# The last 14 weight transfers of each round, split in two by rows

## The reference, cut to what matters

```python
def _moe(h, router_w, router_b, wg, wu, wd):
    logits = (h @ router_w + router_b).astype(jnp.float32)
    top_v, top_i = lax.top_k(logits, MOE_TOPK)
    top_w = jax.nn.softmax(top_v, axis=-1)
    gates = jnp.sum(top_w[..., None] * jax.nn.one_hot(top_i, N_EXPERTS, dtype=jnp.float32), axis=-2)
    out = jnp.zeros_like(h)
    for e in range(N_EXPERTS):
        out = out + gates[..., e:e + 1] * _swiglu(h, wg[e], wu[e], wd[e])
    return out
```

## Time and profile before

| | |
|---|---|
| three runs | 1885.35, 1886.6 and 1887.86 us |
| median | 1886.6 us |
| the profiled execution, first to last instruction | 1888.6 us |
| mean granted clock of PE | 0.974 of full speed |
| PE busy | 1778.0 us, 94% of the span |
| bytes moved | 541.92 MB |

### The profile page before, as it was taken

How to read it: one execution, slowest core, us unless ns; L and a number is a source line. 1 busy time by engine, 2 the same in 40 slices (tenths; PEclk the granted TensorE clock), 3 DMA queues, 4 the chain that set the end, 5 groups by cost and what they waited for, 6 DMA issues and landing times.

```text
span 1888.6 us, 28344 instructions
## 1 busy us (share of the span) xinstructions
PE 1778.0 (94%) x11337; PEld 1307.8 (69%) x11338; DVE 483.9 (26%) x1052; ACT 276.5 (15%) x567; POOL 353.6 (19%) x215
## 2 busy tenths in 40 slices
PE   7999999999999999999999989989999998999896
PEld 4888788778888788888885857565554443444443
DVE  1595535310000286322322001102100100101101
ACT  2104433010000210534011000000000100000001
POOL 2807241569998000000000000000000000000000
PEclk8999999999999999999989999979999999999999
DMA  9745464367765444445458979898998999999994
GB/s 397 259 156 201 151 232 139 129 251 281 266 246 194 177 145 152 134 145 168 178 208 365 416 286 401 346 419 350 418 414 337 412 421 417 419 418 418 416 421 178
DMA packets 86831, 541.92 MB, mean 287 GB/s; under 512 B 8752, under 2 KB 21072, under 8 KB 21840
## 3 DMA queue, kind: packets, MB, share of 16 engines
q1 hardware_dynamic: 67824, 490.24, 65.7%
q0 software_dynamic: 5760, 41.95, 6.0%
q10 hardware_dynamic: 13024, 6.82, 1.2%
HBM read 537.89 MB, written 1.08 MB: 285 GB/s over the span
## 4 chain that ended last, share of the span: by engine, by line
PE 84%; DMA 7%; issue 3%; SPq 2%; DVE 2%; ACT 2%; ACTq 0%; DVEq 0%
PE ps L799 22%; PE ps L1247 12%; PE ps L876 8%; PE ps L893 8%; PE ps L1395 6%; PE ps L1286 6%; PE ps L900 4%; PE ps L1416 3%; PE ps L1325 3%; DMA sq<-in_moe_units 3%; SPq L597 2%; DMA aring<-in_moe_units 2%; DMA misc<-in_moe_units 1%; PE ps L1357 1%; DMA proj<-in_ada_units 1%
## 5 line engine op out<-in xcount | busy, mean ns | idle before, releaser
L799 PE MATMUL ps<-hT,ring 128*128 128x256 f32 x1984 | 438.0, 382 | 1.0 <-ACT hT L1518 1.0
L799 PEld LDWEIGHTS ps<-hT,ring 128*128 128x128 f32 x1984 | 376.7, 191 | 56.1 <-issue 5.1
L701 POOL TENSOR_TENSOR aring<-aring,ccol 128x2048 f32<-128x2048 f32 x40 | 144.5, 3612 | 208.8 <-DVE scan L1941 65.8
L707 POOL TENSOR_TENSOR aring<-aring 128x1024 f32<-128x1024 f32 x80 | 151.3, 1892 | 6.3
L893 PE MATMUL ps<-hT,ring 128*128 128x256 f32 x672 | 146.7, 379 | 0.0
L1247 PE MATMUL ps<-ring,hT 128*64 128x256 f32 (+2 forms) x1152 | 131.7, 364 | 7.8 <-issue 5.6
L893 PEld LDWEIGHTS ps<-hT,ring 128*128 128x128 f32 x672 | 127.0, 190 | 16.9
L1247 PEld LDWEIGHTS ps<-ring,hT 128*64 128x64 f32 (+2 forms) x1152 | 75.0, 133 | 59.5 <-issue 37.9
L2286 DVE TENSOR_TENSOR proj<-proj,ps 128x256 f32<-128x256 f32 (+2 forms) x28 | 14.6, 521 | 352.5 <-PE ps L1247 352.5
L1926 DVE SCALAR_TENSOR_TENSOR misc<-cpad,par,misc 128x256 f32<-128x256 f32 x240 | 102.7, 507 | 0.0
L876 PE MATMUL ps<-proj,ring 128*128 128x256 f32 x384 | 83.2, 379 | 0.0
(11 more groups left out here) (399 smaller groups left out, 1969.0 us busy)
## 6 DMA issues: line engine op xcount, KB each, us to landing
ring<-in_moe_units SPq DMA_DIRECT2D x144, 1024.0 KB, 19.4
ring<-in_dense_units SPq DMA_DIRECT2D x121, 1024.0 KB, 5.0
aring<-in_moe_units SPq DMA_DIRECT2D x48, 1024.0 KB, 18.8
proj<-in_moe_units SPq DMA_DIRECT2D x48, 1024.0 KB, 20.2
aring<-in_ada_units POOLq DMA_DIRECT2D x40, 1024.0 KB, 6.6
extra<-in_moe_units SPq DMA_DIRECT2D x24, 1024.0 KB, 18.2
scan<-in_moe_units SPq DMA_DIRECT2D x24, 1024.0 KB, 21.2
misc<-in_moe_units SPq DMA_DIRECT2D x24, 1024.0 KB, 21.6
```

The lines of the kernel that those rows point to most:

```text
L701: last = g.tensor_tensor(w, w, ccol[:, :].unsqueeze(2).broadcast_to([P, KT, 256]), ALU.mult)
L707: last = g.tensor_tensor(dst, w[:, 0:half_k, :], w[:, half_k:2 * half_k, :], ALU.add)
L799: last = mm(ps[:, n % 2, j * SEQ:(j + 1) * SEQ], wide(s)[:, k, j * P:(j + 1) * P], hT[:, k, :], start=(k == 0), stop=(k == KT - 1))
```

## The change

It concerns the last 14 units of each round, 154 to 167, by `late` 0 to 13. Each is now sent as two transfers, rows 0 to `cut` and rows `cut` to 128, right after one another from the same queue and after the same single wait. `cut` is 8 times the entry of `LOW_ENGINES`: 120, 112, 104, 96, 88, 80, 64, and then seven times 120. Both transfers raise the slot's semaphore by 16, so that the slot counts 13 fills of 16 in a round instead of 12, and `arrived` asks for one more fill for the last unit of each slot. Nothing that is computed changes, nor the bytes that are moved.

```diff
+ENGINES = 16
+LOW_ENGINES = (15, 14, 13, 12, 11, 10, 8) + (15,) * 7
...
-                sp.dma_start(eslot[slot], moe_units[ds(expert, 1), unit].rearrange("e p n -> p (e n)")
-                             ).then_inc(efull[slot], 16)
+                source = moe_units[ds(expert, 1), unit].rearrange("e p n -> p (e n)")
+                late = piece.first_unit + u - (MEMBERS * UNITS - EXP_SLOTS)
+                if late < 0:
+                    sp.dma_start(eslot[slot], source).then_inc(efull[slot], 16)
+                    return
+                cut = P // ENGINES * LOW_ENGINES[late]
+                sp.dma_start(eslot[slot][0:cut, :], source[0:cut, :]).then_inc(efull[slot], 16)
+                sp.dma_start(eslot[slot][cut:P, :], source[cut:P, :]).then_inc(efull[slot], 16)
...
                 def arrived(key):
                     stream = piece.first_unit + AT[key]
-                    pe.wait_ge(efull[stream % EXP_SLOTS],
-                               p * (16 * (MEMBERS * UNITS // EXP_SLOTS)) + 16 * (stream // EXP_SLOTS + 1))
+                    fills = stream // EXP_SLOTS + 1 + (stream >= MEMBERS * UNITS - EXP_SLOTS)
+                    pe.wait_ge(efull[stream % EXP_SLOTS], p * (16 * (MEMBERS * UNITS // EXP_SLOTS + 1)) + 16 * fills)
                     return stream % EXP_SLOTS
```

## The result

| | before | after |
|---|---|---|
| median | 1887.12 us (4 runs, 1885.35 to 1887.86) | 1969.15 us (4 runs, 1964.33 to 1973.41) |
| profiled execution | 1888.6 us | 1969.6 us |

A forecast was written before the change was run, and what follows sets the result against it. Saturated transfers were taken as the bound, with PE following landings and one engine late. Relieving it in the last round gave -6 us, the first round and SP nothing: 1886.6 - 6 = 1880.6 us, range 1877 to 1897.

The forecast's parts named there:

- What bounds the kernel: Expert phase: transfers saturated at 420 GB/s, PE follows the landings, one lone engine works 10 us longer at the end.
- The price of a row: Late units: an 8 KiB row takes an engine 0.312 us, so 14 rows more cost 4.4 us.
- collisions: Rival, late units: two engines write into the same part of on-chip memory and halve each other; slower, chance 0.24.
- midway 3.75 us a unit: Collision rival's price midway between no and all conflicts: a late unit takes 3.75 us instead of 2.5.
- 17.5 us: Collision rival's midway cost for the 14 late units of one round.
- midway case of 1915: Collision rival at its midway price over both rounds: up to +28 us, ending at 1915.
- The first round: First round's late units: 4.4 us more on engines 0 to 7, covered by 5.4 us idle; cost nothing.
- The laggard relieved: Last round: lone engine, if engine 15, loses 80 rows; last landing 5.4 to 9.8 us earlier; chance 0.56.
- rival of the low-numbered laggard: Last round: the lone engine is a low one, gets 14 rows more, ends 4.4 us later (1891.0); chance 0.10.
- How rows are dealt: Late transfers: rows dealt evenly, in order, from the first engine, over as many of 16 as get equal numbers.
- PE and SP: Last round: PE could follow, allowing up to 10.4 us; SP's second issues take 0.33 to 1 us, hidden behind the backlog.
- three signs of being wrong: Profile after: rate under 420 GB/s from 1812 to 1860 or around 1400; lone engine later than 1871; SP's 2 us issues until 1870.

The follow-up runs named there:

- e2: Kernel before with the last 14 units of both rounds each cut at row 64, two even parts: 1.0312 of the kernel before, 59 us slower.
- e5: Kernel before, but in the last round only rows 0 to 63 of the last 14 units sent, as two column halves: 1899.9 us, one run.
- e6: Kernel before, but in the last round only rows 32 to 95 of the last 14 units sent, as two column halves: 1875.2 us, one run.
- e3: The change in the last round alone, first-round units whole, against the kernel before: 1.0238, 45 us slower (1932.1 us).
- e4: The change in the first round alone, last-round units whole, against the kernel before: 1.0220, 42 us slower (1928.4 us).
- e12: Kernel before plus, in the last round, an unneeded copy of eight spaced blocks of 4 rows behind each of the last 14 units: 1.0090, 1904.0 us.
- e13: Kernel before plus, in the last round, an unneeded copy of seven spaced blocks of 4 rows behind each of the last 14 units: 1.0087, 1905.2 us.
- e1: Kernel before with the last 14 units of both rounds each cut by columns into two transfers of 128 rows x 1024 floats: 1.0000 of the kernel before.
- e9: Kernel before plus, in the last round, an unneeded copy of 32 evenly spaced 8 KiB rows behind each of the last 14 units: 1.0036.

## Why the prediction was wrong, point by point

**What bounds the kernel.** Right: saturated transfers, PE behind them, and a lone engine at the end are all as read.

**The price of a row (the step that failed).** The prediction took 0.312 us for each row whatever the pattern (14 x 0.312 = 4.4 us for 14 rows more), a price read from transfers of 128 rows alone, and left collisions to a rival with a chance of 0.24. Split by rows, the packets take about twice as long (165 to 224 GB/s), in e2 with even loads too, and by the place in the on-chip memory they do or don't (e5, e6). At 200 GB/s 14 units take 73 us instead of 35: 38 us more, twice over, are 76 of the 81; e3 and e4 show 45 and 42 us.

**The size of the rival.** Its mechanism was right, its price was not: the midway 3.75 us a unit, with up to +28 us in all, was the dearest case that was priced, and what came was the full conflict, 5 to 6 us a unit. The term "17.5 us" for a round should have been 35 to 45. The range ended at 1897, and so left out even the prediction's own midway case of 1915. There is a slip in its sum too: it turns slower not at 0.4 us a unit but at about 0.23, since 28 units pay and 5.4 + 1.0 us are in hand (28 x 0.23 = 6.4).

**The first round.** The cover was taken as 5.4 us of idle time for a backlog of 4.4. Against a backlog of some 40 us it is nothing, and e4 shows that nearly all of it reaches the end. The idle time was right, the load on it was not.

**The laggard relieved.** Wrong by itself. It was put at engine 15; the changed trace has it alone at about 9 rows a unit, and e12 and e13 slow it from the low side. By the dealing rule it is one of 0 to 6, and neither 15 nor 7, the two that the prediction names. So even without collisions the forecast gain of 6 us would most likely not have come: the rival of the low-numbered laggard, +4.4 us, would have held in its place.

**How rows are dealt.** Right as far as it can be read: the number of engines of every part is confirmed by the packets, and the lone engine has 12 packets a unit in e12 and e13.

**PE and SP.** PE could have followed: in e6, where it does not wait for their landing, it takes 13 of the last units in 24.7 us, 1.9 each. SP's second issues cost nothing that was not hidden (e1 issues as many and loses nothing). But they did not fall to 0.33 to 1 us, as the prediction took them to: the laggard stayed, and in e1 too they run up to 6.1 us.

**The signs.** Of the three signs of being wrong two came: the rate far under 420 GB/s at both places, and the lone engine still there, later than 1871. The third, an unbroken row of 2 us issues until 1870, came in another form, with issues of up to 7.2 us until 1925 that decided nothing.

**What stays open.** The changed kernel loses 22 us more than e2, which collides too. Its uneven loads and its 8-row parts are candidates; no run separates them. That the place in the on-chip memory decides rests on e5 and e6, one run each; how long two engines hold each other up was not measured for a single packet. Why one engine falls behind was not tried, nor which of 0 to 6 it is. No run gives a low engine fewer rows, so whether that would gain the 6 us is open.

## What to carry to other kernels

A transfer's rate depends on which partitions are written at one time, not only on bytes and packet sizes (212 against 328 GB/s in e5 and e6): keep saturated loads at all 128 partitions, and cut them by columns if they must be cut, which was free here. Before work is taken off a slow engine, find out which one it is with a small added load; a forecast that hangs on an engine's number needs a run, not a guess. Where a resource is saturated to the end, a loss far upstream arrives nearly in full (42 us in e4).

## What the runs showed of the hardware that was not expected

- Two transfers of 64 rows x 1024 floats at rows 0 to 63 run at 212 GB/s with the engines busy for 0.87, at rows 32 to 95 at 328 with 0.86. The busy share can't tell a colliding engine from a working one; GB/s over busy share can.
- The same unit in 128 rows runs at 420 GB/s, in 64+64 rows at 220 to 235, in 32 to 95, 0 to 31 and 96 to 127 at 208 to 247.
- The same 256 KiB a unit, from HBM to HBM, cost 0.4% when its 32 rows stood at even distances (16 engines, e9) and 0.9% as 8 spaced blocks of 4 rows (8 engines, e12): the spacing decides over how many engines a copy is dealt, and the packet count of the queue tells it.
- Whole units of 128 rows that are still on their way when the split ones start are slowed as much as these: 5.5 us each for units 147 to 153 of the changed kernel.
